# Dense products that read their moving operand and write their bank from the last column to the first

## The reference

```
h = rmsnorm(x, norm_mix_g)
u = h @ w_in                          # 2048 x 12288, split in ten parts
m = sigmoid(ga) * (ya @ w_a_out) + sigmoid(gb) * (yb @ w_b_out)
x = x + m @ w_o
gate = sigmoid(rmsnorm(x, ple_norm_g) @ w_ple_gate)
x = x + gate * (p @ w_ple_proj)
...
h = rms_norm(x, g) * (1 + scale) + shift
proj = h @ w_in_2                     # split in q, k, v, z of attention and of retention
...
out = y @ w_out_2
x = x + gate * out
```

## Time and profile before

| | |
|---|---|
| executions, median of 3 | 2564.71 us (2564.47 to 2564.88) |
| span of the profiled execution | 2563.3 us |
| TensorE, matmuls | 2548.6 us busy, 99% of the span |
| TensorE, weight loads | 2106.7 us busy, 82%, beside the matmuls |
| VectorE | 1342.8 us busy, 52% |
| ScalarE | 941.9 us busy, 37% |
| DMA | 309.29 MB, mean 121 GB/s |

### The profile page before, as it was taken

How to read it: one execution, slowest core, us unless ns; L and a number is a source line. 1 busy time by engine, 2 the same in 40 slices (tenths; PEclk the granted TensorE clock), 3 DMA queues, 4 the chain that set the end, 5 groups by cost and what they waited for, 6 DMA issues and landing times.

```text
span 2563.3 us, 31667 instructions
## 1 busy us (share of the span) xinstructions
PE 2548.6 (99%) x13058; PEld 2106.7 (82%) x13058; DVE 1342.8 (52%) x2151; ACT 941.9 (37%) x1326; POOL 79.1 (3%) x64
## 2 busy tenths in 40 slices
PE   9999999999999999999999999999999999999998
PEld 8887888887888888888888888888888888888888
DVE  7556734457534555655543363584355545554425
ACT  6543324333323222322232353443344344443423
POOL 0000000000000000000001103200000000000000
PEclk9999999999999999999999999999999999999999
DMA  5322223322234666666443222235312222222424
GB/s 193 110 83 79 87 91 99 91 77 80 92 93 142 220 215 210 217 213 217 144 161 107 99 91 101 96 91 182 98 59 82 84 82 82 74 83 83 166 97 156
DMA packets 159984, 309.29 MB, mean 121 GB/s; under 512 B 11040, under 2 KB 15392, under 8 KB 158816
## 3 DMA queue, kind: packets, MB, share of 16 engines
q1 hardware_dynamic: 159040, 305.70, 36.9%
q0 software_dynamic: 224, 1.15, 0.1%
q10 hardware_dynamic: 576, 0.42, 0.1%
HBM read 298.84 MB, written 8.39 MB: 120 GB/s over the span
## 4 chain that ended last, share of the span: by engine, by line
PE 98%; DVE 2%; ACT 0%; issue 0%; DVEq 0%
PE bank L341 91%; PE bank L1291 1%; PE bank L1292 1%; PE bank L1293 1%; PE bank L810 1%; PE bank L755 1%; PE bank L1457 1%; PE bank L763 0%; PE bank L1631 0%; DVE CGB L2135 0%; DVE EE L460 0%; DVE EE L462 0%; DVE XX L465 0%; DVE XX L455 0%; ACT XX L445 0%; ACT XX L447 0%
## 5 line engine op out<-in xcount | busy, mean ns | idle before, releaser
L341 PE MATMUL bank<-XH,WH 128*128 128x512 f32 (+1 forms) x2880 | 1110.1, 387 | 1.3 <-DVE TMP L1003 0.5
L341 PE MATMUL bank<-XH,WL 128*128 128x512 f32 (+1 forms) x2880 | 1101.9, 385 | 0.0
L341 PE MATMUL bank<-XL,WH 128*128 128x512 f32 (+1 forms) x2880 | 1101.9, 385 | 0.0
L391 DVE TENSOR_TENSOR WL<-RAW,WH 128x1024 fp32r<-128x1024 f32 x443 | 546.2, 1234 | 794.9 <-ACT WH L368 794.0
L368 ACT CAST WH<-RAW 128x1024 fp32r<-128x1024 f32 x443 | 464.0, 1049 | 1061.1 <-PE bank L341 1057.5
L341 PEld LDWEIGHTS bank<-XH,WH 128*128 128x128 f32 x2880 | 540.8, 188 | 111.3 <-DVE TMP L1003 1.3
L341 PEld LDWEIGHTS bank<-XH,WL 128*128 128x128 f32 x2880 | 540.7, 188 | 108.8 <-DVE WL L391 0.2
L341 PEld LDWEIGHTS bank<-XL,WH 128*128 128x128 f32 x2880 | 541.0, 188 | 106.4 <-issue 0.5
L341 PE MATMUL bank<-WH,XH 128*128 128x512 f32 x384 | 150.1, 391 | 0.0
L341 PE MATMUL bank<-WH,XL 128*128 128x512 f32 x384 | 149.5, 389 | 0.0
L341 PE MATMUL bank<-WL,XH 128*128 128x512 f32 x384 | 149.5, 389 | 0.0
(11 more groups left out here) (307 smaller groups left out, 1796.4 us busy)
## 6 DMA issues: line engine op xcount, KB each, us to landing
RAW<-in_w_in SPq DMA_DIRECT2D x303, 512.0 KB, 3.6
AST<-in_w_ada SPq DMA_DIRECT2D x192, 256.0 KB, 4.1
RAW<-in_w_out SPq DMA_DIRECT2D x40, 512.0 KB, 3.4
RAW<-in_w_o SPq DMA_DIRECT2D x32, 512.0 KB, 3.6
RAW<-in_w_gate SPq DMA_DIRECT2D x32, 512.0 KB, 3.4
RAW<-in_w_a SPq DMA_DIRECT2D x16, 512.0 KB, 4.2
RAW<-in_w_b SPq DMA_DIRECT2D x16, 512.0 KB, 4.2
XT<-in_xT SPq DMA_DIRECT2D x4, 1024.0 KB, 6.8
```

What stands on the lines that cost most here:

```text
L341: ins = nc.tensor.matmul(bank[b][:, cols], l, r[:, cols], start=first, stop=final)
L391: nc.vector.tensor_tensor(WL[:, m % NSPL], RAW[:, m % NRAW], WH[:, m % NSPL].bitcast(F32), ALU.subtract).then_inc(lo.sem, lo.step(m))
```

## The change

It is one line. The moving operand and the bank are each given a step of -1 along the columns, so that column 511 (or 255 of a half) is read and written first and column 0 last. Both are turned, so each product ends up in its own place. The stationary operand, the number of matmuls, their sizes, flags, waits and signals stay as they were.

```diff
                     first, final = q == 0 and j == 0, q == nk - 1 and j == 2
-                    ins = nc.tensor.matmul(bank[b][:, cols], l, r[:, cols], start=first, stop=final)
+                    ins = nc.tensor.matmul(bank[b][:, cols][:, ::-1], l, r[:, cols][:, ::-1], start=first, stop=final)
                     done = [(name, i)] * (j == 2 and q == nk - 1)
```

## The result

The changed kernel takes 2627.97 us (median of three executions, 2627.25 to 2628.29), against 2564.71 us before: a ratio of 1.0244, with a 95% interval of 1.0229 to 1.0258. It is 63.3 us slower. The profiled execution has a span of 2627.0 us, 63.7 us more than before.

The account below looks back on a forecast made before the run. TensorE's stream of dense matmuls was taken as the bound (10272 x 0.2268 + 384 x 0.120 = 2376 us, 93% of the span). Reading and writing backwards were taken as zero, so 2565 us stayed; range 2560 to 2707 us.

Parts of the forecast that it names:

- What bounds the kernel: Whole kernel: TensorE's stream of matmuls sets the time; dense pitches add to 2376 us, 93% of the span.
- Reading backwards: Moving read of the dense matmuls: claimed not tied to neighbours in rising order, from line 755's medians; cost taken as zero.
- Writing backwards: Bank writes of the dense matmuls: no row showed them; turned columns still come in neighbouring pairs, cost assumed zero.
- Half pace: Rival, moving read or bank write: each column needs its own access, 0.82 ns per column, 4667 us; chance 0.15.
- A fixed price: Rival, start or last pair of each turned stream: some ns more per matmul, at most 142 us, 2707 us; chance 0.12.
- The fixed part shrinks: Rival, dense matmuls: turned order might avoid the moving read hindering the next weight load; at most 2423 us, chance 0.05.
- the 13.3 ns: Part of each dense matmul's 226.8 ns pitch left after 512 columns at 0.417 ns, claimed the same whatever the width.

Follow-up runs that it names:

- e5_forms: Second kernel of matmul streams alone, without the computation, with varied read orders and stationary widths: forward 226.7 ns, falling pieces of 4 columns 233.3 ns at 512 columns.
- e7: Kernel before, with dense products reading the moving operand in pieces of 4 columns, pieces falling, columns inside rising, banks written in rising order: 2627.41 us, ratio 1.0242.
- e9: Fourth kernel of fp32r matmul streams alone, moving and stationary tiles shifted against each other: forward 226.7 ns at distance 0, turned 233.3 to 233.5 at 15 of 17 distances.
- e12: Changed kernel (moving operand and bank turned) with every tile from `XH` on moved 32 bytes up: 2627.05 us, ratio 1.0242.
- e11: Kernel before, all products forward, with every tile from `XH` on moved 32 bytes up: 2625.3 us, ratio 1.0236.

## Why the prediction was right, and where it was not

The forecast was no change at 2565 us with a chance of 0.68. It did not come true. By the prediction's own sign, a pitch of line 341 that moves by more than 0.5 ns, it was wrong: the pitch moved by 6.6. The measured 2628 us lies in the range of 2560 to 2707 us, because the range took in the second of the slower cases, the price of some ns per matmul, which had a chance of 0.12. That is luck more than insight, since no row stood behind this price or behind its bound of 13.3 ns.

**What bounds the kernel** was read rightly. Nothing but the pitch of 10656 dense matmuls decided. 6.6 ns on the long pieces and 4 to 6 on the short ones make up the 63.3 us, with no cover and no side effect on another engine.

**Reading backwards** is the step that failed. The text took from the 182/183 ns of line 755 that the order of the moving read is free. It named the weakness, that these are plain float32 matmuls with 0.82 ns per column, and then did not let it count. The runs show that it was decisive: in plain float32 a turned read costs nothing at 512 columns (429 ns both ways) and a step of 2 costs 21 ns, 0.04 ns per column, which is 0.7 ns in 16 columns and can't be seen in rows 6 and 7. In fp32r the same step of 2 doubles the matmul (453 ns against 226.7).

**Writing backwards** was the side for which no row spoke, and it is free: 2564.6 us. The rule of the Trainium skill cited there, in "Advanced Engine Details and Errata", section Memory Cachelines, says that a non-contiguous pattern slows matmuls significantly. A step of -1 did not; whether the rule counts it as contiguous the page doesn't say. Its other half asks for at least two hits on a 16-byte line in SBUF. For fp32r the runs go against that: one of every two columns has two hits per line and takes 453 ns, and 2 of every 4 takes 451 ns.

**Half pace** did not come. Of what it named, a turned pair costs nothing: a stream whose pairs rise with their two columns exchanged takes 226.7 ns (e5_forms), and so do fours turned inside 16 bytes.

**A fixed price** was right in its size, between 0.5 and 13.3 ns, and wrong in its kind. It was to be the same at every width, and it is +6.6 ns at 512 columns, 0 at 320 and -1.6 at 256. Its place was put at the start or the last pair of a stream; e5 and e7 put it in the order of the 16-byte pieces of the read, and e9 to e12 tie its size at 512 columns to where the two tiles lie that TensorE reads beside each other.

**The fixed part shrinks** was taken from the 13.3 ns per matmul, with the sentence that nothing in the trace links the moving read and the weight load. They are linked: the stationary tile's place moves the pitch from 226.7 to 233.3 ns. (The Trainium skill leans the same way as the text did: "TensorE: Matmul & The Clock Gate", section Step-by-step: what each phase is for, has two independent read ports, so that a weight load doesn't steal read bandwidth from the running matmul. In fp32r e9 and e11 show the running matmul's pitch changed by where the loaded tile lies; whether bandwidth is what it loses isn't shown.) One column read again and again takes 215.8 ns in place of 226.7. The 13.3 ns are no constant. The kernel before already stood at the best distance found for 512 columns, so what the text priced as a possible gain was there to lose.

No version beats the kernel before by an amount that can be measured. At 256 columns the best distance has 113.8 ns in place of 120, which on 384 matmuls would be 2.4 us, under the 5.1 us that count as a difference here; it wasn't tried in the kernel.

## What to carry to other kernels

When TensorE's pitch is the bound, a few ns of it are worth per cents, and they can hang on addresses. For fp32r with 512 columns, allot moving and stationary tiles so that their starts differ by a multiple of 256 bytes (at 256 columns another distance was better, so measure there), read the moving operand in whole pieces of 16 bytes that follow each other in rising order, and turn the output if something must be turned, since that is free. Before an order of reading is called free by a row of the trace, see that the row is of the same type and runs at the same pace per column: a stream with slack hides what a stream without it pays.

## What the runs showed of the hardware that was not expected

- The pitch of a 512-column fp32r matmul is 226.7 ns when the moving and the stationary tile lie a multiple of 256 bytes apart (or with one at column 0 and the other at column 60), and 229 to 237 ns otherwise. Moving every tile from `XH` on by 32 bytes, with no other edit, makes this kernel 60 us slower.
- A turned read has 233.3 ns or more at each of 17 distances. bf16 and plain float32 with 512 columns don't see the turn at all.
- A shorter stationary tile makes a forward matmul slower, not faster: 226.7 ns with 128 columns, 230.0 with 96 and 64, 231.7 with 32.
- Streams of 192 and of 128 columns have the same pitch, 111.4 and 111.3 ns, so there it is not the number of moving columns that sets it.
